# Hybrid decoder trunk on one core: expert rows through DRAM, a turned tile moved into a product, and four waits rearranged

## The reference

```python
p = rmsnorm(h, e_norm_mix) @ e_w_in           # pooling groups | spatial gating u, v
h = h + concat([pool_mixer(a_in), u * (tril(ws) @ layernorm(v) + bias)]) @ e_w_out
h = h + swiglu(rmsnorm(h, e_norm_ffn), wg, wu, wd)
xn = rmsnorm(h, o_norm_mix); xx = shift(xn) - xn
xr, xw, xk, xv, xa, xg = [xn + xx * mu[i] for i in range(6)]   # RWKV-7 from these
h = h + rwkv7(...)
xt = rmsnorm(h, o_norm_ffn)
gates = softmax over the two largest of xt @ router            # top 2 of 8
for e in range(8):
    h = h + gates[:, e:e+1] * (silu(xt @ wg[e]) * (xt @ wu[e])) @ wd[e]   # width 3584
out = rmsnorm(h, final_norm)
```

## Time and profile before

| | us |
|---|---|
| median of 3 runs | 1616.0 (1615.29 to 1616.95) |
| the profiled execution, its own time | 1617.56 |
| its span, first to last instruction | 1615.7 |
| PE busy | 1557.3 (96%) |
| DVE busy | 1232.3 (76%) |
| ACT busy | 965.2 (60%) |
| chain that ended last: PE | 95% |
| expert jobs | from 613.9, one every 123.2 |

### The profile page before, as it was taken

The page is one execution under the profiler, slowest core; times in us unless marked ns, Lnnn a source line. Parts: engine busy times, 40 slices in busy tenths (PEclk is TensorE's granted clock), DMA queues, the critical chain, the costliest instruction groups (busy, mean ns, idle before and its releaser), DMA issues.

```text
span 1615.7 us, 21885 instructions
## 1 busy us (share of the span) xinstructions
PE 1557.3 (96%) x8072; PEld 1300.8 (81%) x8072; DVE 1232.3 (76%) x1477; ACT 965.2 (60%) x1107; POOL 5.9 (0%) x9
## 2 busy tenths in 40 slices
PE   6999999699999989999999999999999999999996
PEld 4779999478889847888888888888888888888885
DVE  3335544621777248999999999999999999999997
ACT  2234443230232226887887887887887887887884
POOL 0000000000000000000000000000000000000000
PEclk9999999799999999999999999999999999999999
DMA  9449543211003547999999999999998998999960
GB/s 353 156 156 278 185 157 129 80 38 67 25 1 106 183 157 282 376 371 324 378 377 323 372 373 327 370 369 330 373 374 326 369 376 325 375 370 325 374 241 26
DMA packets 192951, 424.17 MB, mean 263 GB/s; under 512 B 6882, under 2 KB 31714, under 8 KB 192771
## 3 DMA queue, kind: packets, MB, share of 16 engines
q1 hardware_dynamic: 190834, 420.94, 72.0%
q10 hardware_dynamic: 1776, 1.45, 0.3%
q0 software_dynamic: 288, 1.05, 0.2%
HBM read 422.38 MB, written 1.05 MB: 262 GB/s over the span
## 4 chain that ended last, share of the span: by engine, by line
PE 95%; DVE 2%; DMA 1%; ACT 1%; issue 1%; DVEq 0%; ACTq 0%; POOL 0%
PE psum L1377 19%; PE psum L1379 19%; PE psum L1378 19%; PE psum L537 7%; PE psum L2007 4%; PE psum L2008 4%; PE psum L2009 4%; PE psum L1358 2%; PE psum L1957 2%; PE psum L811 2%; PE psum L1998 2%; PE psum L1395 2%; DMA work<-e_pool_w_dram 1%; PE psum L614 1%; PE psum L697 1%; PE psum L707 1%
## 5 line engine op out<-in xcount | busy, mean ns | idle before, releaser
L1537 DVE TENSOR_TENSOR w_lo<-ring,w_hi 128x1024 fp32r<-128x1024 f32 x672 | 804.5, 1222 | 43.8 <-ACT w_hi L1468 4.0
L1468 ACT ACTIVATE w_hi<-ring 128x1024 fp32r<-128x1024 f32 x672 | 711.5, 1062 | 181.0 <-PE psum L1379 180.8
L1377 PE MATMUL psum<-w_hi,xg_split 128*128 128x512 f32 x896 | 354.3, 395 | 3.6 <-DVE xg_split L1629 3.6
L1379 PE MATMUL psum<-w_lo,xg_split 128*128 128x512 f32 x896 | 350.1, 391 | 0.0
L1378 PE MATMUL psum<-w_hi,xg_split 128*128 128x512 f32 x896 | 349.3, 390 | 0.0
L1377 PEld LDWEIGHTS psum<-w_hi,xg_split 128*128 128x128 f32 x896 | 168.7, 188 | 37.5 <-DVE xg_split L1629 3.8
L1379 PEld LDWEIGHTS psum<-w_lo,xg_split 128*128 128x128 f32 x896 | 168.5, 188 | 35.8
L1378 PEld LDWEIGHTS psum<-w_hi,xg_split 128*128 128x128 f32 x896 | 168.9, 188 | 33.6
L1377 PE MATMUL psum<-w_hi,ht_split 128*128 128x512 f32 x448 | 175.1, 391 | 0.0
L1379 PE MATMUL psum<-w_lo,ht_split 128*128 128x512 f32 x448 | 174.4, 389 | 0.0
L1378 PE MATMUL psum<-w_hi,ht_split 128*128 128x512 f32 x448 | 174.3, 389 | 0.0
(11 more groups left out here) (297 smaller groups left out, 1607.2 us busy)
## 6 DMA issues: line engine op xcount, KB each, us to landing
ring<-o_moe_wg_dram SPq DMA_DIRECT2D x56, 2048.0 KB, 7.9
ring<-o_moe_wu_dram SPq DMA_DIRECT2D x56, 2048.0 KB, 8.6
ring<-o_moe_wd_dram SPq DMA_DIRECT2D x56, 2048.0 KB, 8.0
ring<-e_ffn_wg_dram SPq DMA_DIRECT2D x11, 1024.0 KB, 5.5
ring<-e_ffn_wu_dram SPq DMA_DIRECT2D x11, 1024.0 KB, 8.8
ring<-e_ffn_wd_dram SPq DMA_DIRECT2D x11, 1024.0 KB, 11.3
ring<-e_w_in_dram SPq DMA_DIRECT2D x2, 2048.0 KB, 18.0
ring<-e_w_out_dram SPq DMA_DIRECT2D x2, 2048.0 KB, 25.5
```

The lines of the kernel that those rows point to most:

```text
L1377: nc.tensor.matmul(dst, x_hi, hi, start=first, stop=False)
L1379: return nc.tensor.matmul(dst, x_hi, lo, start=False, stop=last_)
L1468: nc.scalar.activation(w_hi[:, (4 * i + n) % 4, :], piece(i, n), ACT.Copy).then_inc(m_hi, 1)
L1537: V.tensor_tensor(w_lo[:, r, :], piece(i, n), w_hi[:, r, :].bitcast(F32), ALU.subtract).then_inc(m_lo, 1)
```

## The change

Each token's normed row, now already times the norm gain (loaded into `gain` by ACT, multiplied in `router_rows`), is written into a DRAM tensor `expert_rows` of 16 blocks of 128 rows. The block and row are the expert and the token's rank in it (`row_at`). POOL writes them by four indirect DMAs before job 0; the tensor is cleared with zeros during the FFN. SP loads a job's block, already in order, while the previous job runs. PE turns it by eight transposes (`rows_turned`); ACT and DVE split it from psum by halves. The first job still uses `gather`. The last activation tile of a job is turned between the two halves of the next-to-last down product. Outside the jobs: `ws` is turned after the next product; the RWKV mixes follow the difference by quarters, with PE waiting for each; tables for Sqrt are loaded early (`root_table`); the final norm works by halves and SP and ACT write the output.

```diff
 moe_pe:
+def rows_turned(j):
+    pe.wait_ge(x_in, j * 16 + 16)
+    for k in range(KT):
+        last = nc.tensor.transpose(psum[:, 2 + k // 4, ...], rows_in[:, k * P:(k + 1) * P], ident)
+        if k % 4 == 3: last.then_inc(m_ga, 1)
 ...
     if c >= 1: turned(j, c - 1)
+    if c == NEC - 1: rows_turned(j)
     hidden(j, 1, c)
-    if c >= 1:
+    if c == NEC - 1:
+        down(j, c - 1, (0, 1))
+        turned(j, c)
+        down(j, c - 1, (2, 3))
+    elif c >= 1:
         down(j, c - 1)
-turned(j, NEC - 1)
-pe.wait_ge(m_p, j + 2)
-gather(pe, 0)
-gather(pe, 1)
 down(j, NEC - 1)
 moe_act, at load ("d", NEC - 1):
+    consumed(act, j, ("u", NEC - 1))
+    gathered(j * 2 + 2)          # two copies of 512 columns from psum
+    pieces_hi(j, i, True, (0,))
+    turned(NEC - 1)
+    pieces_hi(j, i, True, (1, 2, 3))
 moe_dve:
+    if (what, c) == ("d", NEC - 2):
+        pieces_lo(j, i, (0, 1, 2)); gated(NEC - 1); pieces_lo(j, i, (3,))
+    elif (what, c) == ("d", NEC - 1):
+        gathered(j * 2 + 2)      # two subtracts of 512 columns from psum
+        pieces_lo(j, i, (0,)); turned(NEC - 1); pieces_lo(j, i, (1, 2, 3))
-    (eight tensor_scalar into XG by col("o_norm_ffn", k), then one 1024-wide subtract)
+    (row_at: nine small operations after the first one-hot)
 moe_sp:
+def rows(j):
+    sp.wait_ge(m_ga, j * 2 + 2)
+    at = sp.value_load(jobs[0:1, bass.ds(j + 1, 1)], ...)
+    sp.dma_start(rows_in, ...rows_dram block at...).then_inc(x_in, 16)
     (after load 14 of each job; in job 0 after x_put >= 64)
 moe_pool:
+for i in range(2 * TB):
+    nc.gpsimd.indirect_dma_start(rows_dram, IndirectOffsetOnAxis(row_at[:, i:i + 1], 0), xn3[:, i % TB, :], None)
 FFN loads on SP:
+if c == 1:
+    sp.wait_ge(x_zero, 1)
+    sp.dma_start(rows_dram (all 2048 rows), zero_rows broadcast).then_inc(x_clear, 16)
 RWKV entry:
+for i, (l, r) in enumerate(lhs_rhs): pe.wait_ge(mix_ready, KT * mixed + i + 1)   # products 0 to 2
+def stepped(q): ...  xx of columns 2q, 2q+1
+mixed(0): stepped(k // 2) before k = 0, 2, 4, 6; each mix increments mix_ready
 even layer on PE:
-pe.wait_ge(s_small, 80); four transposes of ws
     slot_in[1]; turned_product(w8(1), g, 4 + g) for g in range(4)
+pe.wait_ge(s_small, 80); four transposes of ws
 router_rows:
-norm_rows(dve, 3, b)
+reciprocal; xn3[:, b, :] = h[:, b, :] * small * gain   (scalar_tensor_tensor, after ng_in)
 end, per block b:
+ACT: Square of h by halves, each with its own sum; Sqrt
+DVE: two small operations, reciprocal, h = h * small * gain (block 1 by halves)
+SP writes block 0, ACT writes block 1 in two halves
```

More of the change, by code:

```diff
@@ L200, in trunk @@
         f_phi, f_plo, f_pc = sem("ffn_pieces_hi"), sem("ffn_pieces_split"), sem("ffn_pieces_used")
-        s_out = sem("out_written")
+        s_out = [sem(f"out{i}_written") for i in range(3)]
         s_dbg = sem("dbg")
@@ L539, in product @@
                 return last
[L542 to L547, removed]
+            product(0, [(w1s[:, k, :], mix[0][:, k, :]) for k in range(KT)], 64, mixed=0)
+            product(1, [(a1s[:, k, :], mix[1][:, k, :]) for k in range(KT)], 64, mixed=1)
+            product(2, [(g1s[:, k, 0:P], mix[2][:, k, :]) for k in range(KT)], mixed=2)
             product(3, [(g1s[:, k, P:160], mix[2][:, k, :]) for k in range(KT)], 32)
@@ L868, in gn_mean, with root_table @@
             last.then_inc(gn_m, 1)
+        def root_table():
+            nc.scalar.activation(small[:, 501:502], small[:, 4:5], ACT.Sqrt)
         def rwkv_act(act):
+            root_table()
             norm_act(act, 2)
@@ L1004, in mixed @@
                 for k in range(KT):
[L1005 to L1008, removed]
+                    if j == 0 and k % 2 == 0:
+                        stepped(k // 2)
+                    nc.vector.scalar_tensor_tensor(out=mix[j][:, k, :], in0=xx[:, k, :],
+                                                   scalar=col("o_mu", 8 * MIX[j] + k), in1=xnT[:, k, :],
+                                                   op0=ALU.mult, op1=ALU.add).then_inc(mix_ready, 1)
             def copies(dst, n0):
@@ L1472, in moe_act, with gathered @@
             nc.scalar.activation(tb_["ex"], tb_["d"], ACT.Exp).then_inc(r_exd, 1)
-            act.wait_ge(m_xf, 1)
-            nc.scalar.activation(xg_split[:, 0, :, :], r3(XG, KT), ACT.Copy).then_inc(m_xh, 1)
+            def gathered(n):
+                for q in range(2):
+                    act.wait_ge(m_ga, n + q + 1)
+                    nc.scalar.activation(xg_split[:, 0, 4 * q:4 * q + 4, :], r3(psum[:, 2 + q, :], 4), ACT.Copy).then_inc(m_xh, 1)
+            gathered(0)
             def outputs(j):
@@ L1614, in onehot, with gathered @@
                     g_ = gt[:, b, bass.ds(col_, 1)]
[L1615 to L1630, removed]
+                    last = V.tensor_scalar(Pg[:, b * P:(b + 1) * P], C("iota"), r_, g_, ALU.is_equal, ALU.mult)
+                last.then_inc(m_pg, 1)
+            def gathered(n):
+                for q in range(2):
+                    dve.wait_ge(m_xh, n + q + 1)
+                    last = V.tensor_tensor(xg_split[:, 1, 4 * q:4 * q + 4, :], r3(psum[:, 2 + q, :], 4),
+                                           xg_split[:, 0, 4 * q:4 * q + 4, :].bitcast(F32), ALU.subtract)
+                last.then_inc(m_xg, 1)
             def scattered(j, o=0):
@@ L1949, in _ @@
                         last.then_inc(p_in, 1)
-            pe.wait_ge(s_small, 80)
-            for g in range(4):
-                last = nc.tensor.transpose(psum[:, 2, g * P:(g + 1) * P], r3(E_["ws"], 4)[:, g, :], ident)
-            last.then_inc(s_wsT, 1)
             def turned_product(w, g, bank):
@@ L1972, in _ @@
                 turned_product(w8(1), g, 4 + g)
+            pe.wait_ge(s_small, 80)
+            for g in range(4):
+                last = nc.tensor.transpose(psum[:, 2, g * P:(g + 1) * P], r3(E_["ws"], 4)[:, g, :], ident)
+            last.then_inc(s_wsT, 1)
             pe.wait_ge(slot_in[2], 16)
```

151 lines of the change are left out of this document (115 added, 36 removed).

## The result

The changed kernel takes 1576.9 us (median of 4 runs, 1576.7 to 1578.5) against 1615.6 us (1614.7 to 1617.0) before: ratio 0.976, 95% interval 0.9745 to 0.9779. The forecast was 1578.6. The profiled execution took 1577.18 us (span 1575.3), 40.4 us less than the one before. The text calls the profile's DVE VectorE, its ACT ScalarE and its POOL GpSimd.

What follows compares the result with a forecast made beforehand. PE was taken to bound the kernel, DVE and DMA close behind. 20.0+7.3+4.9+2.4+2.8=37.4 us off the profiled 1617.56 gave 1580.2, as median 1578.6 us; forecast's own range 1573 to 1583, with smaller rival losses 1572 to 1590.

Steps and rivals of the forecast that it cites:

- The jobs: Eight expert job ends: gather products leave PE, transposes come in, net 2.5 us a job, 20.0 us gained (12 to 21.5).
- T=0: Zero of the job-end timeline: PE ends the last up product; turned tile complete at 5.82 us, PE wants it at 5.88.
- rival A: Job ends: the turned tile stalls PE 1.0 us a job instead of 0.2, total 1585 us; chance 0.13.
- The start: Before the output projection: PE no longer idles for small loads, nor runs at half clock after; 7.3 us (6.3 to 7.6).
- the RWKV entry: RWKV layer's first products: early root table and mixes by quarters let PE start sooner, 4.9 us gained (3 to 6.3).
- The router: Router and first gather: less work after the gather, shorter PE pause, half the clock loss counted; 2.4 us (1.2 to 3.4).
- The tail: Final norm and output: no table load, work by halves, last write issued earlier; 2.8 us gained (1.8 to 3.7).
- B: Jobs: DMA becomes the bound; at 365 GB/s each job takes 122.1 us, total 1590 us; chance 0.09, covering the 358 GB/s rule.
- The clear: Zeros written between FFN chunks 1 and 2: 22 us, costing nothing; rival at 100 GB/s: 1625 us, chance 0.05.
- The terms around the table load: Square-root table load taken off the path: 0.95 us at the RWKV entry, 1.28 us in the tail.

## Why the prediction was right

**The jobs** (20.0, measured 20.4). The ledger from T=0 came out to 0.1 us at every step, and the wait at its end was 0.1 us where I had taken 0.2. What I had understated was the weight of that placement: I priced a stalled tile at 1.0 us a job (rival A, 1585), but with both orders undone it is 3.3 us and then the clock, and the kernel falls back to 1614. The edit is not "gather out, transposes in": with only PE's order undone 7 of the 20.4 us are left, with both undone less than none.

**The start** (7.3, measured 7.2) and **the RWKV entry** (4.9, measured 5.0) hold, and the first of them holds with its share for the clock. Undone they cost 8.8 and 5.0. The feed-forward layer's 1.2 us were not in the sum: its cold stretch at the entry ended at 93.7 instead of 103, on an entry 7.2 us earlier, so half-clock products lasted 3.5 us instead of some 6. It did not come back with the start undone (that stretch ended at 99 on an entry at 96). The traces of the experiments tell more. From PE's start on the output projection to this layer's end it is 223.1 us before and 221.9 after. In six further kernels whose half clock at the entry lasted 3.4 us it is 221.7 to 221.9, with the start undone or not; in two whose PE program is that of the changed kernel up to there, but whose half clock lasted 6.8 us as before the change, it is 222.3 (PE's order undone) and 222.7 (doubled zeros). So the 1.2 us go with the length of that fall, which differs where the program does not, and that they came was luck. The start's own 7.2 are good to about half a microsecond: the same projection began between 56.2 and 57.4 us in kernels that are alike up to there. The 8.8 us between medians there is 5.6 between the profiled executions. The other three executions of that kernel had a mean clock of 0.985 to 0.986 and not 0.988, worth about 3 us by estimate; where it fell no trace shows.

**The router** (2.4, measured 3.0). I counted half of the 1.7 us for the clock's fall behind the first gather. No fall came, since the granted clock is 1.00 from 596 on: the other 0.85 us, less a wait of 0.17 us for a piece that stood behind VectorE's list of jobs, and less 0.09 us more for the norm with its gain.

**The tail** (2.8, measured 3.7, its upper bound). The second of the last block's half writes is issued at 1572.7, which is 2.4 us earlier than before once the 36.7 us gained up to there are taken off, as forecast (1609.4 for 1611.79). From that issue to the end of the span it is 2.6 us, where it was 3.9; a half write of 256 KB landed after 2.1 us and the whole one of 512 KB, which GpSimd issued, after 3.2. The forecast had this too, with its 2.7 us of landing, but summed it wrongly: 1609.4+2.7=1612.1 is 3.6 us before 1615.7, and not 2.8. The terms around the table load are smaller than I had them: 0.86 and 0.6 us, not 0.95 and 1.28.

**The rivals.** A and B did not occur, but B is now bounded: 396 GB/s can be had, so the demand of 370 stayed under it, although had shown me 369 and I had read that as a capacity. It was a demand. The 358 GB/s of the Trainium skill (DMA: Bandwidth & Descriptors, Bandwidth), which would have made it 1609, lie 10% below what this core moved for 800 us. The same section gives 358 GB/s for two cores of one HBM domain that stream together and 425 for a core alone, and this kernel runs on one core: I took the wrong one of the two. The clear took 29.8 us from issue to landing and not 22: 3 MB of loads issued in the 2.5 us before it were still under way, and 401 GB/s were moved over the whole of it, 422 to 423 once only zeros were left.

```profile
70.00:75.00 5.00, 5.00 (x13) 2.20 (x12) 1.76 (x4) 2.63 (x4) 0.00 (x0) 1.00 1.03 423
```

The slack hid it, as it hid twice as much.

## What to carry to other kernels

Before work is taken off the bounding engine, ask what hides behind it: here the gather covered the split of a tile, and with it taken out and the tile left at its old place the jobs were slower; the gain came from putting other products there and from the place of one subtraction in VectorE's queue. When you price a wait, walk through the waiting engine's whole queue and not only its next instruction, and look at the granted clock behind it. A bandwidth read in a stretch where nothing waits for DMA is a demand and no capacity; load it with more to see the limit. When you price a term, add it up once more from its parts: the tail's sum was off by 0.8 us.

## What the runs showed of the hardware

- Of eight waits of 3.3 us of PE, five were followed by about 3.4 us at half clock and three were not; no wait of 1.5 us was. The same kernel took from 1611.8 to 1624.9 us, at mean clocks from 0.983 down to 0.974.
- The clock also fell without a pause of PE: from 317 to 331 us and from 316 to 333, in products over 64 rows and the transposes behind them, in two of the three kernels in which PE had been kept busy earlier. Which condition brings it on stays open.
- One core moved 396 GB/s of loads for 800 us while more was asked for, and 411 to 423 GB/s while zeros were written to DRAM from one broadcast tile. An output write of 256 KB issued by ScalarE landed after 2.1 us, one of 512 KB after 2.6 us when SP issued it and after 3.2 us when GpSimd did.
- Four indirect scatters of 128 rows of 4 KB each took GpSimd 0.95 to 1.95 us each to issue, and nothing waited for them.
